# Value evictions shared between two engines, gate sums held in PSUM, convolution taps placed anew, and the first head of an mLSTM block in another order

## The reference

```python
x_m, z, glu_a, glu_b = jnp.split(h @ w_in, 4, axis=-1)
x_c = silu(causal_depthwise_conv(x_m, w_conv_m, b_conv_m))       # 4 taps
q, k, v = x_c @ w_q, x_c @ w_k, x_m @ w_v                        # by head
gates = concat(q, k, v) @ w_gates + b_gates
ig, lf = gates[..., :H], log_sigmoid(gates[..., H:])
b = cumsum(lf)                                                   # per head
w = exp(b_t - b_s + ig_s - m_t), causal;  m_t = b_t + running max of (ig - b)
h_m = ((q k^T) * w / 16) v / max(|row sum|, exp(-m_t))
a = causal_depthwise_conv(glu_a * sigmoid(glu_b), w_dw, b_dw)    # 31 taps
a = silu(group_layer_norm(a, 8, g_cn, b_cn))
y = concat(sigmoid(z) * group_layer_norm(h_m), a) @ w_out
```

## Time and profile before

| | |
|---|---|
| median of 3 runs | 2276.02 us (2275.9 to 2280.16) |
| the profiled execution | 2276.22 us, of which the span from the first to the last instruction is 2274.4 |
| mean granted TensorE clock | 0.993 |
| PE busy | 2221.9 us (98%) |
| DVE, POOL, ACT busy | 1248.2, 1113.6, 985.0 us |

### The profile page before, as it was taken

One profiled execution on the slowest core, in us unless ns is written; L12 is line 12 of the kernel. 1 busy time (PEld: TensorE's weight loads), 2 busy tenths in 40 slices (PEclk: granted clock), 3 DMA queues, 4 the chain that ended last, 5 costly groups with the idle time before them and its releaser, 6 DMA issues.

```text
span 2274.4 us, 28719 instructions
## 1 busy us (share of the span) xinstructions
PE 2221.9 (98%) x10450; PEld 1750.4 (77%) x10450; DVE 1248.2 (55%) x2077; ACT 985.0 (43%) x1614; POOL 1113.6 (49%) x596
## 2 busy tenths in 40 slices
PE   7999999999999999999999999999999999999998
PEld 5886667788888878766778888887767688888886
DVE  4989846863556599984464122147776653221222
ACT  3368543333133335775343223234666653331323
POOL 2688833544344648875364444363322244443442
PEclk9999999999999999999999999999999999999999
DMA  8432205354656323220222323332212123323232
GB/s 318 138 94 75 67 29 162 129 203 145 237 173 204 93 80 97 75 85 28 65 75 93 101 93 97 97 95 78 77 55 65 47 93 93 103 92 98 96 98 87
DMA packets 206662, 240.39 MB, mean 106 GB/s; under 512 B 9762, under 2 KB 172378, under 8 KB 206554
## 3 DMA queue, kind: packets, MB, share of 16 engines
q1 hardware_dynamic: 205990, 238.76, 33.0%
q10 hardware_dynamic: 564, 0.21, 0.0%
HBM read 236.84 MB, written 2.10 MB: 105 GB/s over the span
## 4 chain that ended last, share of the span: by engine, by line
PE 83%; DVE 7%; POOL 3%; ACT 3%; issue 2%; DMA 1%; ACTq 0%; DVEq 0%; POOLq 0%; SPq 0%
PE product L2507 25%; PE product L2509 25%; PE product L2508 25%; PE product L2880 1%; POOL ring_low L950 1%; PE side L2864 1%; PE side L3075 1%; POOL slot_f L981 1%; PE product L3110 1%; DVE side L1884 1%; PE side L3095 1%; POOL slot_f L1003 1%; DMA ring_f<-in_w_out 1%; ACT ring_high L1076 1%; DVE side L1672 1%
## 5 line engine op out<-in xcount | busy, mean ns | idle before, releaser
L950 POOL TENSOR_TENSOR ring_low<-ring_f,ring_high 128x1024 fp32r<-128x1024 f32 (+1 forms) x349 | 842.5, 2418 | 1045.6 <-ACT ring_high L1076 1045.0
L2507 PE MATMUL product<-slot_r,ring_high 128*128 128x512 f32 (+1 forms) x2536 | 1006.1, 397 | 14.0 <-POOL ring_low L950 6.0
L2509 PE MATMUL product<-slot_r,ring_high 128*128 128x512 f32 (+1 forms) x2536 | 989.2, 390 | 0.0
L2508 PE MATMUL product<-slot_r,ring_low 128*128 128x512 f32 (+1 forms) x2536 | 988.4, 390 | 0.0
L1076 ACT ACTIVATE ring_high<-ring_f 128x1024 fp32r<-128x1024 f32 (+1 forms) x349 | 367.7, 1056 | 707.4 <-DMA ring_f<-in_w_ff 329.9
L2507 PEld LDWEIGHTS product<-slot_r,ring_high 128*128 128x128 f32 (+1 forms) x2536 | 475.9, 188 | 143.7 <-issue 30.7
L2509 PEld LDWEIGHTS product<-slot_r,ring_high 128*128 128x128 f32 (+1 forms) x2536 | 475.9, 188 | 101.9
L2508 PEld LDWEIGHTS product<-slot_r,ring_low 128*128 128x128 f32 (+1 forms) x2536 | 476.3, 188 | 97.0 <-issue 1.4
L1884 DVE SCALAR_TENSOR_TENSOR side<-slot_f,cols,side 128x512 f32<-128x512 f32 x380 | 253.5, 749 | 0.6
L1842 DVE SCALAR_TENSOR_TENSOR va<-product,sqt 128x512 f32<-128x512 f32 x96 | 66.3, 692 | 333.3 <-ACT sqt L1154 332.0
L1862 DVE TENSOR_TENSOR slot_f<-product,slot_f 128x512 f32<-128x512 f32 x64 | 44.2, 690 | 175.1 <-PE product L2509 175.1
(11 more groups left out here) (324 smaller groups left out, 2077.2 us busy)
## 6 DMA issues: line engine op xcount, KB each, us to landing
ring_f<-in_w_ff SPq DMA_DIRECT2D x128, 512.0 KB, 3.8
slot_f<-in_w_ada SPq DMA_DIRECT2D x48, 1024.0 KB, 7.2
ring_f<-in_w_in SPq DMA_DIRECT2D x96, 512.0 KB, 3.9
ring_f<-in_w_out SPq DMA_DIRECT2D x40, 512.0 KB, 3.4
ring_f<-in_w_up SPq DMA_DIRECT2D x32, 512.0 KB, 3.7
ring_f<-in_w_down SPq DMA_DIRECT2D x32, 512.0 KB, 3.7
slot_f<-in_x SPq DMA_DIRECT2D x4, 512.0 KB, 5.2
ring_f<-in_w_v SPq DMA_DIRECT2D x4, 512.0 KB, 3.5
```

What stands on the lines that cost most here:

```text
L950: pool.tensor_tensor(whole(ring_low[:, s, :, :], n), whole(ring_f[:, s, :, :], n), whole(ring_high[:, s, :, :], n).bitcast(F32), ALU.subtr ...
L2507: pe.matmul(out_ap, high, rhs_high, start=start, stop=False)
L2508: pe.matmul(out_ap, low, rhs_high, start=False, stop=False)
L2509: return pe.matmul(out_ap, high, rhs_low, start=False, stop=stop)
```

## The change

- **Values.** In each layer ACT evicts value tiles 0 and 1; DVE copies 2 to 7 and takes each head's `xc_low` one step later.
- **Gate sums.** `gb` is no longer a row of the SBUF region but lies over `glf` in PSUM (PM[1]). ACT copies the input gates out of PSUM into `a_row` behind its softplus, and DVE subtracts `gb` in place.
- **Taps, first layer only.** `cut` puts 5 taps of tiles 4, 5 ahead of `glu(3)` (4 before) and 7, 2, 2, 2 into the four gaps (7, 2, 1, 0 before), so 13 are left (17 before). `bias_gates`, `gate_rows` and the centrings stand at later taps of tiles 6, 7.
- **End of the z products.** `conv_mean(6)` and `(7)` stand before `gate_product(7)`, both `conv_vars` behind it. ACT squares tiles 6 and 7 before it evicts z tile 6, and takes the group deviation before `decay(0, j)`.
- **First head.** `conv_spreads(0)` comes before the first weighted values and `conv_spreads(2)` before the second, both into PB[2] and PB[3] (`spread_bank`); DVE refines before `weighted(0, 0)` and normalises in pairs between the weighted scores. `conv_product(0)` waits for 4 normalised tiles where it waited for 6.

```diff
-        a_row, gate_parts, gu, gb = (region_f[0:n, SE + k * T:SE + (k + 1) * T]
-                                     for k, n in ((3, HEADS), (4, P), (5, HEADS), (6, HEADS)))
+        a_row, gate_parts, gu = (region_f[0:n, SE + k * T:SE + (k + 1) * T]
+                                 for k, n in ((3, HEADS), (4, P), (5, HEADS)))
-        glf = PM[1][0:HEADS, :]
+        glf = gb = PM[1][0:HEADS, :]
...
-        lsig_ready = Signal(sem("softplus_ready"), 1)
+        lsig_ready = Signal(sem("softplus_then_input_gates_ready"), 2)
...
         def spread_bank(t):
-            return (PB[2], PB[3], PM[2], PM[3])[t % 4]
+            return (PB if t < BLK else PM)[2 + t % 2]
...
                         ahead.of(place, I_V + hd // 2)
+                        if hd == 0:
+                            o = O_V + t
+                            wait_done(act, place, LAYER, o)
+                            wait_taken(act, place, O_XM + t)
+                            act.activation(xm(t, CONV_M - 1, T), bank(o)[:], ACT.Copy).then_inc(taken[o % 4].sem, 1)
                         if 5 + t < NT:
                             silu_short(5 + t)
...
                 act.activation(gu, gu, ACT.Ln, bias=one_col[0:HEADS]).then_inc(lsig_ready.sem, 1)
+                wait(act, place, ig_done, 1)
+                act.activation(a_row, input_gates, ACT.Copy).then_inc(lsig_ready.sem, 1)
...
+                    if t == 6:
+                        conv_square(6)
+                        conv_square(7)
                     act.activation(tile(SE, t), bank(o)[:], ACT.Sigmoid).then_inc(taken[o % 4].sem, 1)
...
                 taps.make(place, TAPS)
-                conv_square(6)
-                conv_square(7)
+                square_root_next()
+                wait(act, place, cvar, 2)
+                deviation(place, PM[2][:, 0:P], P, croot_ready)
...
                     decay(0, j)
-                square_root_next()
-                wait(act, place, cvar, 2)
-                deviation(place, PM[2][:, 0:P], P, croot_ready)
...
-                    long_conv(place, 4, 0, 4)
+                    long_conv(place, 4, 0, 5)
...
-                cut = (4, 11, 13, 14, 14, 17) if l == 0 else (12, 19, 22, 24, 26, 28)
+                cut = (5, 12, 14, 16, 18) if l == 0 else (12, 19, 22, 24, 26)
...
-                for hd in range(HEADS):
+                for hd in range(1, HEADS):
                     for t in (2 * hd, 2 * hd + 1):
...
                         dve.tensor_copy(xm(t, CONV_M - 1, T), bank(o)[:]).then_inc(taken[o % 4].sem, 1)
-                    xc_low(2 * hd, 2 * hd + 1)
+                    xc_low(2 * hd - 2, 2 * hd - 1)
+                xc_low(6, 7)
...
-                    wait(dve, place, ig_done, 1)
-                    steps.did(dve.tensor_tensor(a_row, input_gates, gb, ALU.subtract))
+                    wait(dve, place, lsig_ready, 2)
+                    steps.did(dve.tensor_tensor(a_row, a_row, gb, ALU.subtract))
...
-                    long_conv(place, 6, beside={2: bias_gates, 9: gate_rows, 14: lambda: centre_conv(0, 1),
-                                                18: lambda: centre_conv(2, 3), 22: lambda: centre_conv(4, 5)})
+                    long_conv(place, 6, beside={8: bias_gates, 13: gate_rows, 22: lambda: centre_conv(0, 1),
+                                                27: lambda: centre_conv(2, 3)})
+                    centre_conv(4, 5)
...
                 diagonal(0)
-                weighted(0, 0)
-                weighted(0, 1)
                 wait(dve, place, croot_ready, 1)
                 settled(dve)
                 refine(PM[2], P, P, crn_small)
+                weighted(0, 0)
+                weighted(0, 1)
                 wait(dve, place, cxc_ready, NT)
+                conv_normed(0, 1)
                 weighted(0, 2)
+                conv_normed(2, 3)
                 weighted(0, 3)
-                conv_normed(0, 1, 2, 3)
                 conv_low(0)
...
                 gate_product(6)
-                gate_product(7)
                 conv_mean(6)
                 conv_mean(7)
+                gate_product(7)
                 conv_vars(0)
+                conv_vars(1)
...
-                        elif t < 4:
+                        elif t in (4, 5):
                             wait(pe, place, p_ready, BLK)
                         else:
-                            wait(pe, place, cy_ready, t - 3)
+                            wait(pe, place, cy_ready, t - 1)
...
                     if c == 0:
-                        wait(pe, place, cy_ready, NT - 2)
+                        wait(pe, place, cy_ready, BLK)
...
                 stabiliser(0)
-                conv_vars(1)
                 scores(0, 0)
                 scores(0, 1)
+                conv_spreads(0)
                 wait(pe, place, vc_ready, BLK * HEADS)
...
                 weighted_values(0, 0)
                 scores(0, 2)
+                conv_spreads(2)
                 weighted_values(0, 1)
                 scores(0, 3)
-                conv_spreads(0)
                 weighted_values(0, 2)
-                conv_spreads(2)
                 stabiliser(1)
                 conv_spreads(4)
                 weighted_values(0, 3)
```

## The result

| | before | after |
|---|---|---|
| median of 9 runs each | 2276.4 us (2274.87 to 2280.16) | 2282.7 us (2281.36 to 2288.6) |
| ratio, 95% interval | 1 | 1.0031 (1.0023 to 1.0039) |
| span of the profiled execution | 2274.4 us | 2279.8 us |
| mean granted TensorE clock | 0.993 | 0.989 |

What follows compares the result with a forecast made beforehand. TensorE, busy 2221.9 of 2274.4 us, was taken as the bound, so only its waits could shrink. First layer +0.55 and second -2.45 made -1.9, from 2276.02 to 2274.3 us; 8-in-10 range 2268.3 to 2278.3.

Steps and rivals of the forecast that it cites:

- rival B: Clock falls to half rate at the pause before the first weighted values: 2275.3 to 2285.8 us; chance 0.14.
- the wait for POOL in the first layer: At the first weighted values, PE waits 3.6 us (2.5 to 5.3) for POOL's last values.
- The 1.2 us waits ahead of the last spreads: In each layer, `conv_spreads(6)` waits for normalised tile 5: a new wait of 1.2 us (0 to 1.9).
- Values: Value chunks and low parts: ACT's copies and the later `xc_low` gain 1.6 us a layer (0.8 to 2.1).
- Gate rows: DVE's gate rows last 5.7 us instead of 7.7, with four `floor_rows` at 1.2 instead of 3.13.
- the 0.64: PE's wait for `floor_rows`, 0.64 us, goes in both layers.
- Taps: First layer only: earlier taps gain 1.2 us; later centrings bring POOL's last values to 281.4 to 282.1.
- the wait at L2806: First layer: PE's 1.0 us wait for the convolution of tiles 6 and 7 goes.
- Rival A: POOL is not late in the first layer, so the 3.6 us wait goes: 2270.7 us, or 2268.3; chance 0.27.
- First head: From weighted values to convolution product: -1.1 - 0.27 + 1.2 = -0.17 us, and -0.75 at L2582, in each layer.
- The 1.7 at L2582: PE's wait at head 1 falls from 1.7 to about 1.0 us: -0.75 (0 to -1.7) a layer.
- Rival C: POOL's low part holds the value chunk and `floor_rows` stay at 3.13: 2275.9 to 2277.9 us; chance 0.12.

Runs made afterwards that it cites:

- tap 23: The changed kernel with the first layer's centrings of tiles 2 and 3 at tap 23, not 27: 2277.8 us, ratio 1.0003 to the kernel before.

## Why the prediction was wrong

The step that failed is the choice between the forecast and rival B. The clock's fall had a chance of 0.14, of which 0.04 beyond what can be measured. The argument for so little was the pause of 2.75 us in the earlier trace rows, at which the clock had held. And only one place was priced, the wait for POOL in the first layer. The 1.2 us waits ahead of the last spreads stood in the sum by their length alone, in both layers, and the wait at head 1 was not seen. The runs showed four low stretches, worth 8.9 us. The forecast's -1.9 and these 8.9 make +7.0; the two mixers cost 6.7. So close a fit is partly chance, but filling the pauses takes the ratio back from 1.0031 to 0.9999, and the sign that the prediction named, a clock at 0.5 behind the wait for POOL, is there. The trace of before also has a nearer row than that of 1676. Right behind the first mixer, after waits of 0.54 and 0.52 us for VectorE among narrow matmuls, it shows a low clock without any long pause:

```profile
426.00:428.00 2.00, 1.48 (x9) 1.40 (x9) 1.67 (x11) 0.91 (x2) 1.11 (x1) 0.59 1.05 392
```

The other steps, by the trace:

- Values, 1.6 us a layer: mis-sized. In the run with them alone the four matmuls of above are shifted by -1.2, -3.5, -2.1 and -4.4, which is 2.3 a layer. "PE is then held by POOL until 178.03" was wrong, as the first row below shows: PE starts at 174.52 without a wait, when POOL's low part of 174.29 has just begun. The whole 2.75 us hung on the copy. In return the four low parts in a row take 8.18 us, not the 7.2 of two slow pairs, and PE waits 1.34 for them, which the sum had at nothing.
- Gate rows: `floor_rows` take 1.22 as counted, and the 0.64 is gone. From the first of the gate rows at 226.77 to their end at 232.9 there are 6.1 us, not 5.7.
- Taps: the wait at L2806 is gone. The last centring of tile 3 ended at 253.8 and POOL's values at 279.74, some 2 us sooner than counted, 1.2 of it because this execution is that much ahead before the mixer. PE came as much sooner, and the wait was right: 3.52 for 3.6. Rival A is out.
- First head: the waits are 1.43 (1.2 counted) and 0.34 for `refine` (0.2 counted). The 1.7 at L2582 went wholly, but 1.49 and 0.45 came ahead of it, for VectorE's weighting.

Timelines after, of TensorE, VectorE and GpSimd, by engine:

```profile
174.52 0.47 PE L2518 MATMUL product<-slot_r,ring_high 128*128 128x512 f32 x1
...
190.88 0.50 PE L2518 MATMUL product<-slot_r,ring_high 128*128 128x512 f32 x1 [1.34 <-DVE slot_r L2018]
...
177.85 1.28 DVE L2018 TENSOR_TENSOR slot_r<-slot_f,slot_r 128x512 fp32r<-128x512 f32 x2
...
182.65 8.18 DVE L2018 TENSOR_TENSOR slot_r<-slot_f,slot_r 128x512 fp32r<-128x512 f32 x4
...
226.77 0.69 DVE L2068 SCALAR_TENSOR_TENSOR side<-side,slot_f 4x512 f32<-4x512 f32 x1 [0.81 <-ACT slot_f L1322]
...
252.56 1.28 DVE L2086 SCALAR_TENSOR_TENSOR slot_f<-side,slot_f 128x512 f32<-128x512 f32 x2
...
174.29 2.41 POOL L950 TENSOR_TENSOR ring_low<-ring_f,ring_high 128x1024 fp32r<-128x1024 f32 x1
...
184.04 3.45 POOL L981 TENSOR_TENSOR slot_f<-slot_f,va 128x512 f32<-128x512 f32 x2
187.45 2.83 POOL L950 TENSOR_TENSOR ring_low<-ring_f,ring_high 128x1024 fp32r<-128x1024 f32 x1
...
276.13 3.61 POOL L1003 TENSOR_SCALAR slot_f<-slot_f,small 128x256 f32<-128x256 f32 x4
```

Without the clock the first layer comes to 6.7 - 5.9 = +0.8 (forecast +0.55) and the second to -3.0 (forecast -2.45). The bookkeeping of waits came out near, and was of no use for the sign. In the first layer this is partly luck: the values gained 0.7 more than counted and L2582 1.0 more, and the wait at head 1, which was not counted, took back 1.2. Rival C is out: both parts did what they say.

The Trainium skill (TensorE: Matmul & The Clock Gate, section "HAM oscillation — how this bites in real kernels") describes pauses between bursts of matmuls that bring the clock down each time. The filled pauses of this case agree with it, at 1.00 with and 0.50 without. Its example is a kernel that waits for its DMAs at each step; here the clock fell behind a wait of 0.83 us for VectorE as well.

## What to carry to other kernels

Price a new wait of TensorE by what runs behind it at half clock too, not by its length alone: here pauses of 3.5, 1.4, 1.5 and 1.4 us cost 8.9 us on top of themselves. Read PE's busy time and the granted clock beside the list of waits: where busy time grows with the same instructions, look at the clock; here it was that. Look in the trace of before for all places where the clock is already low, and at how short the pauses ahead of them are. If a pause can't be removed, matmuls into a bank that is overwritten anyway can keep the clock up, as they did here.

## What the runs showed of the hardware

- The length of a pause does not decide alone. The clock held through 2.75 us between full products and through 1.72 us behind weighted values. It fell at 5.04 us behind full scores, at 1.49 us behind a product of 4 rows, and at 1.43 and 0.83 us ahead of the last spreads of 32 rows, with earlier spreads and one small weighted value in front of the pause. Spreads without a pause of such length did not bring it down (0.99 from 275 to 286 with tap 23). The neighbours do not decide alone either: late in the second layer, at a wait of 2.01 us (values alone) and of 2.09 us (with gate sums) between full products and spreads, the clock held in the first and fell in the second. No run varied the spreads at a fixed pause, so what decides stays open. The windows of the two kernels, in this order:

```profile
1118.00:1120.00 2.00, 1.50 (x32) 0.93 (x28) 0.00 (x0) 0.75 (x1) 0.00 (x0) 1.00 0.35 122
1118.00:1120.00 2.00, 1.83 (x17) 1.30 (x18) 0.20 (x1) 0.55 (x1) 1.37 (x1) 0.50 0.00 0
```

- VectorE's four low parts with two SBUF operands took 8.18 us beside POOL's work (the rows at 184.04 and 187.45), where another pair took 1.28. The Trainium skill (SBUF — State Buffer, section "Who interferes with whom") has the rule that a VectorE instruction with two SBUF inputs and a GpSimd instruction that reads SBUF get in each other's way; the rows agree, and `floor_rows` with one operand in PSUM fell from 3.13 to 1.22.
